# State product of each group issued one z piece ahead, with five smaller moves in the order of VectorE, ScalarE and GpSimd

## The reference, cut to what matters

```python
u = rms_norm(h, norm_mix)
z, xbc, dt_raw, q_a, c_kv, k_rope, gate_ssd, gate_mla = split_cols(u @ w_in)
# xbc: convolution, silu, split into xs (2048), B and C (4 groups x 128)
# 4 groups of 8 heads of 64, 2 chunks of 128 tokens:
cb      = C . B                          # per group and chunk, 128 x 128
y_diag  = (cb * exp(a_cum_l - a_cum_s) for s <= l) . (x * dt)
state   = B . (decay_to_end * x * dt)    # of chunk 0, 128 x 512 per group
y_off   = exp(a_cum) * C . state         # into chunk 1
y       = (y_diag + y_off + d_skip * x) * silu(z)
y       = y * rsqrt(mean(y * y per group) + eps) * ssd_norm
y_ssd   = y @ w_ssd_out
merged  = sigmoid(gate_ssd) * y_ssd + sigmoid(gate_mla) * y_mla
```

## Time and profile before

| | |
|---|---|
| median of 3 runs | 1092.04 us (1090.55 to 1095.19) |
| the profiled execution's own time | 1089.01 us |
| its span, first to last instruction | 1087.2 us |
| PE busy | 1011.7 us, 93% of the span |
| DVE, ACT, POOL busy | 621.3, 517.4, 19.4 us |
| mean granted TensorE clock | 0.981 |
| the stage of the change, end of z 1 to start of so 1 | 113.2 to 212.3 us of the span |

### The profile page before, as it was taken

How to read it: one execution, slowest core, us unless ns; L and a number is a source line. 1 busy time by engine, 2 the same in 40 slices (tenths; PEclk the granted TensorE clock), 3 DMA queues, 4 the chain that set the end, 5 groups by cost and what they waited for, 6 DMA issues and landing times.

```text
span 1087.2 us, 19436 instructions
## 1 busy us (share of the span) xinstructions
PE 1011.7 (93%) x8574; PEld 932.8 (86%) x8574; DVE 621.3 (57%) x828; ACT 517.4 (48%) x701; POOL 19.4 (2%) x24
## 2 busy tenths in 40 slices
PE   7999989899999999999997768699999999999998
PEld 6999878799889999998765545389999999999998
DVE  6798677765565893544111110079994765555566
ACT  5576577745556573542211110168567563443453
POOL 0000020001000000000000000000000000000000
PEclk9999999999999999998999888899999999999999
DMA  7666342346224456499999999775320366555431
GB/s 280 249 221 228 117 188 91 148 166 233 78 78 162 171 197 251 168 387 381 412 420 420 422 419 421 310 294 194 127 107 34 132 232 210 183 190 194 169 141 40
DMA packets 34872, 240.97 MB, mean 222 GB/s; under 512 B 4064, under 2 KB 4448, under 8 KB 6368
## 3 DMA queue, kind: packets, MB, share of 16 engines
q1 hardware_dynamic: 33264, 232.54, 56.0%
q0 software_dynamic: 1232, 6.99, 1.7%
q10 hardware_dynamic: 288, 0.15, 0.1%
HBM read 238.58 MB, written 1.08 MB: 220 GB/s over the span
## 4 chain that ended last, share of the span: by engine, by line
PE 69%; DMA 11%; DVE 11%; ACT 6%; issue 2%; SPq 1%; DVEq 0%; ACTq 0%
PE ps L462 16%; PE ps L463 16%; PE ps L464 16%; DMA wr<-in_c_weights 8%; DVE wlo L1976 4%; PE ps L535 3%; PE ps L1225 3%; DMA T<-in_c_weights 2%; ACT whi L1324 2%; PE ps L1191 1%; PE ps L928 1%; DMA raw<-in_c_weights 1%; SPq L2945 1%; PE ps L1252 1%; PE ps L1265 1%
## 5 line engine op out<-in xcount | busy, mean ns | idle before, releaser
L1976 DVE TENSOR_TENSOR wlo<-raw,whi 128x2048 fp32r<-128x2048 f32 (+1 forms) x119 | 269.4, 2267 | 134.2 <-ACT whi L1324 134.0
L462 PE MATMUL ps<-XUh,whi 128*128 128x256 f32 x992 | 280.8, 283 | 8.6 <-DVE wlo L1976 7.7
L463 PE MATMUL ps<-XUl,whi 128*128 128x256 f32 x992 | 276.9, 279 | 0.0
L464 PE MATMUL ps<-XUh,wlo 128*128 128x256 f32 x992 | 276.9, 279 | 0.0
L1324 ACT ACTIVATE whi<-raw 128x2048 fp32r<-128x2048 f32 (+1 forms) x119 | 223.5, 1882 | 64.0 <-PE ps L464 61.6
L462 PEld LDWEIGHTS ps<-XUh,whi 128*128 128x128 f32 x992 | 188.6, 190 | 10.7 <-issue 8.3
L463 PEld LDWEIGHTS ps<-XUl,whi 128*128 128x128 f32 x992 | 187.4, 189 | 0.3
L464 PEld LDWEIGHTS ps<-XUh,wlo 128*128 128x128 f32 x992 | 187.0, 189 | 0.0
L1225 PE MATMUL ps<-wr,Xg 128*32 128x256 f32 x480 | 55.2, 455 | 20.1 <-DMA wr<-in_c_weights 10.9
L2867 DVE SCALAR_TENSOR_TENSOR sphs<-sphs,wsl,ps 128x256 f32<-128x256 f32 x8 | 3.8, 481 | 94.7 <-ACT sphs L1941 94.7
L1225 PEld LDWEIGHTS ps<-wr,Xg 128*32 128x32 f32 x480 | 29.2, 130 | 32.4 <-issue 28.6
(11 more groups left out here) (621 smaller groups left out, 2368.7 us busy)
## 6 DMA issues: line engine op xcount, KB each, us to landing
raw<-in_c_weights SPq DMA_DIRECT2D x139, 1024.0 KB, 4.9
wr<-in_c_weights SPq DMA_DIRECT2D x36, 1024.0 KB, 26.3
xhi<-in_c_weights SPq DMA_DIRECT2D x12, 1024.0 KB, 26.0
xlo<-in_c_weights SPq DMA_DIRECT2D x12, 1024.0 KB, 26.4
extra<-in_c_weights SPq DMA_DIRECT2D x10, 1024.0 KB, 27.4
acb<-sums POOLq DMA_DIRECT2D x4, 1024.0 KB, 4.7
T<-in_c_weights SPq DMA_DIRECT2D x4, 1024.0 KB, 24.8
T8b<-in_c_weights SPq DMA_DIRECT2D x4, 1024.0 KB, 26.0
```

The costliest lines, as they stand in the source:

```text
L462: pe.matmul(ps, h(k), xh(k), start=start and k == 0, stop=False, skip_group_check=loose)
L463: pe.matmul(ps, h(k), xl(k), start=False, stop=False, skip_group_check=loose)
L464: t = pe.matmul(ps, l(k), xh(k), start=False, stop=stop and k == kt - 1, skip_group_check=loose)
L1976: dve.tensor_tensor(l[:, 0:n], r, h[:, 0:n].bitcast(F32), ALU.subtract).then_inc(*did("w_lo", "split", i))
```

## The change

- PE: `s0 g` is issued after z 2g+2 instead of after z 2g+3, for groups 0 to 2. Group 3 keeps its place.
- DVE: for groups 1 and 2 the state copy moves ahead of the products `M` by `CB`; for groups 0 and 3 it keeps its place. The lower half `upcoming("z", 2g+1)` moves ahead of `CB` for groups 1 to 3.
- ACT: the table load stands ahead of the wait for `dte`; the silu of groups 0 and 1 (`gate_y(0)`) comes one step later, behind the upper half of z 6 and the evacuation of z 4; `ya_root(3)` comes ahead of the upper half of so 1.
- DVE: `ya_add(2)` comes ahead of the lower half of gs 3.
- POOL: the product of group 1 waits for `m0` of group 2 too.

```diff
@@ pe_program, ssd @@
                 t.then_inc(*did("ssd_pe", "cb", g))
                 yield
-                yield
                 ps, free = bank.take("s0", g)
                 w.wait_ge(*free)
                 w.wait_ge(*at_("ssd", "xw", g))
                 w.wait_ge(*at_("emptied", "btok"))
                 pe.matmul(ps[:, :], Btok[:, g, :], xw[:, :]).then_inc(*did("ssd_pe", "s0", g))
+                yield
                 if g == 3:
                     yield
@@ act_program, ssd @@
             for g in range(4):
+                table(LOGEXP)
                 w.wait_ge(*at_("ssd", "dte_in", g))
-                table(LOGEXP)
...
                 act.activation(M[:, 1, :, :], M[:, 1, :, :], ACT.Exp, scale=-1.0).then_inc(*did("ssd_act", "ssd", "e", g, 1))
+                yield
                 if g == 1:
                     gate_y(0)
-                yield
                 yield
@@ act_program @@
         ya_upper(2)
+        ya_root(3)
         upcoming("gate_ssd", 3)
-        ya_root(3)
         ya_upper(3)
@@ dve_program, ssd @@
+            def state(g):
+                w.wait_ge(*at_("s0", g))
+                dve.tensor_copy(S0[:, :], bank.ps("s0", g)[:, :]).then_inc(*bank.emptied("s0", g))
+
             for g in range(4):
+                if g:
+                    upcoming("z", 2 * g + 1)
                 w.wait_ge(*at_("cb", g))
...
                 t.then_inc(*did("ssd_dve", "ssd", "m0", g))
-                upcoming("z", 2 * g + 1)
+                if g == 0:
+                    upcoming("z", 1)
+                if g in (1, 2):
+                    state(g)
                 if g == 3:
                     ya_add(0)
                     ya_add(1)
...
                 yield
+                if g in (0, 3):
+                    state(g)
                 yield
-                w.wait_ge(*at_("s0", g))
-                dve.tensor_copy(S0[:, :], bank.ps("s0", g)[:, :]).then_inc(*bank.emptied("s0", g))
                 if g == 3:
                     yield
@@ dve_program @@
         ya_scale(1)
+        ya_add(2)
         upcoming("gate_ssd", 1)
-        ya_add(2)
@@ pool_program @@
             if g == 3:
                 gate_y(0)
+                w.wait_ge(*at_("ssd", "m0", 2))
                 gate_y(1)
```

## The result

The changed kernel took 1076.01 us in the median of 4 runs (1071.06 to 1078.36), the kernel before 1092.22 in 4 runs beside them: ratio 0.9851, 95% interval 0.9816 to 0.9887. The profiled execution took 1077.94 (span 1076.1) against 1089.01 (span 1087.2), so 11.1 less.

A forecast was written before the change was run, and what follows sets the result against it. Mostly bound by TensorE work, with only PE's waits to be gained: 1.25 + 2.15 + 2.90 + 1.42 + 0 + 1.49 = 9.2 us, so a median of 1092.0 − 9.2 = 1082.8 us, range 1079 to 1087.5.

The forecast's parts named there:

- Point 1: State product ahead, its copy ahead of M by CB: gains 1.25 us ahead of z 3 and 2.15 in y.
- −2.15 (1.74, 0.2, 0.2): Waits for the state copy inside y 1, y 0 and y 2, taken to go whole: 2.15 us gained.
- 16.25: One group's PE work without waits, in us, from two starts of the state product less a wait of 0.20.
- Point 2: Earlier lower half and table load, POOL's product of group 1 held: the wait ahead of z 7 goes, 2.90 us gained.
- Point 3: Half clock in z 7, behind the wait of 2.90, goes: 1.42 us gained, bounds 0 and 1.42.
- 7.8: Gain in us if the clock term is worth nothing and the rest holds, giving 1084.2; a rival at 15%.
- Point 4: `ya_add(2)` earlier: group sum 2 loses its 1.32 us wait, group sum 3 waits 1.65 instead of 0.33; net 0.
- Point 5: `ya_root(3)` ahead of the upper half of so 1: the 2.23 us wait in so 0 shrinks by 1.49, to 0.7.
- DVE did not become the bound in groups 1 and 2: Rival, 12%: state copy or POOL's product delays DVE in groups 1 and 2; 5.2 us gained, 1086.8.
- the tail did not give back: Rival, 10%: squares, roots and lower halves set so 0 whatever the order; 6.5 us gained, 1085.5.
- later stages absorbed nothing of the 11: Rival, 5%: the later memory-bound stage ends when it did before; 1 to 3 us gained, 1090.
- less half clock in the stage, not more: Rival, 3%: TensorE falls to half clock in the stage more often than before; slower, 1100 us with three pieces.

The follow-up runs named there:

- late_copy: Changed kernel with only the DVE state copies of groups 1 and 2 moved back behind the lower halves of z 6 and gs 0: stage 90.75 us against 88.03.
- no_lower: Changed kernel with the lower half put back behind M for groups 1 to 3: 1072.97 us in one run, stage 88.28.
- no_act_pool: Changed kernel with the table load, silu and POOL product moves undone, state product and lower half still early: 1085.49 us in one run, stage 93.25.
- no_root: Changed kernel with the root of group 3 back behind the upper half of so 1: 1075.37 us in one run, stage 89.50.
- packed: Changed kernel with the tail of the stage also reordered on ACT and DVE: 1075.04 us, ratio 0.9881 to the kernel before, stage 86.26.
- again_before: The kernel before, unchanged, run again with its own trace: ratio 0.9962 against itself, 12 runs with a median of 1088.25 us, stage 100.61.
- no_state: Changed kernel with the state product and its copy put back on PE and DVE: 1083.27 us, ratio 0.9923 to the kernel before, stage 91.92.
- only_state: Kernel before with only the moves of the state product and its copy: 1086.06 us, ratio 0.9928 to the kernel before, stage 93.67.

## Why the prediction was right or wrong

**Right: what the change does, and that it lasts.** The state product stands behind z 2, z 4 and z 6, no wait is left from z 3 to gs 1, the clock is full, `dte` takes 0.15 and no table load follows it. The 11.1 of the two profiled executions are kept to the end of the kernel.

**Point 1, the state product, was mis-sized: here the forecast failed in the profile.** "−1.25" is right. "−2.15 (1.74, 0.2, 0.2)" reads the brackets as the cost of the waits. They cost 2.14 + 1.13: `late_copy` shows 0.38 on top for each. The same 0.38 sat in the 16.25 us that I took for one group's work without waits: I took off the bracket of 0.20 alone. In the changed kernel two starts of the state product lie 15.66 apart. The trace of before held it already, since y 3, which waits for nothing, lasts 3.11 from first start to last end, and y 0 3.70 with a bracket of 0.20. I had compared the waits, not the blocks. So y 1 began 2.0 earlier and y 2 8.9 earlier, measured from cb 0, where the forecast had 1.4 and 7.7; y 0 began 1.2 earlier, as forecast.

**Point 2.** −2.90 came, and `M` by CB was held for 0.36 where I took 0.6. The reason I gave first, the earlier lower half, is worth only 0.25 (`no_lower`); the table load, the silu and the POOL product together carry 5.2 (`no_act_pool`). The additions of y 1 took 0.48 each, under POOL's product and outside it, so 0 for them was right.

**Point 3, the half clock, was right for this profile, and one draw of several.** No half clock is left in the stage. The −1.42 itself was not measured apart; by the spacing of z 7 it is 1.4 to 1.6. I set the sum against the median as if all executions of before had one fall there, and gave the Trainium skill's rule only the chance of a smaller gain, 7.8. Three traces show that the kernel before has three waits behind which the clock may fall in the stage, and that one, two or three of them did: stages of 99.12, 100.27 and 100.61. The changed kernel has none of them, in four traces. The rule of the Trainium skill (TensorE: Matmul & The Clock Gate, part 1) that the gate follows recent activity, counted from instants that don't follow the kernel, agrees with that; I had applied it in one direction only. The mean gain of the stage is 12.0, but at the start of the expert stage it is 11.0, so the further falls of the stage don't explain the median in these traces.

**Point 4.** 0 was right: group sum 2 lost its 1.32 and group sum 3 waits 1.73 instead of 0.33, where 1.65 was forecast. No run undoes this move alone.

**Point 5.** −1.49 was forecast, the wait inside so 0 went from 2.23 to 0.75, and `no_root` costs 1.47.

**Not in the sum at all:** the 0.67, of which some 0.4 is the cheaper state product of groups 1 and 2 and the rest the chance of the spacing, and the small wait at group sum 0, 0.22.

**From 11 to the median.** 9.2 + 1.13 + 0.67 + 0.1 for the small waits is 11.1, and that is what the two profiled executions differ by. Over all runs, 53 of before have a median of 1091.4 and 17 of the changed kernel 1077.9, so 13.4 less. The 2.4 between the 11.0 at the expert stage and these 13.4 I can't place. Single runs spread by 12 us in the one and by 10 in the other, and the first four of the changed kernel, 1076.01, lay 2.6 below the median of its thirteen later ones. So of the 16.2 between the first medians 11 are shown to be the stage, and 2.8 are gone again when all runs are taken. With 11.1 in place of 9.2 the forecast would have been 1081, inside the range. What put the time outside it is the step from the sum of one profile to a median. The low end, 1079, was made from point 4 and part of the waits left in place, with no room for a wait that costs more than its bracket, and it took the scatter from three runs, 4.6, where seventeen show 12.4.

**The rivals.** None came. DVE did not become the bound in groups 1 and 2 (y 2 waits for nothing), the tail did not give back, later stages absorbed nothing of the 11, and there was less half clock in the stage, not more. But the 1 us or so beyond the 11, and the 1.8 of `packed`, did not reach the expert stage.

## What to carry to other kernels

Price a wait by the block that it stands in, with and without the wait, not by its bracket: among small matmuls a wait of 0.2 us cost 0.6. Where the clock falls behind a wait in the one trace you have, count every wait of that size as one behind which it may fall, and look at several traces before you set a sum against a median; and follow the difference to a later point of the kernel, since what `again_before` lost to the clock in one stage was made good by the expert stage. When a product is made earlier, ask what its inputs now stand behind: with the state product and the lower half early, but table load, silu and GpSimd's product where they were, it waited 2.33 us for its `xw`, and the stage took 5.2 more.

## What the runs showed of the hardware

- A wait inside a run of 64-column products cost 0.37 to 0.39 us beyond its bracket, for brackets from 0.20 to 1.74 (kernel before, `no_state`, `late_copy`, `only_state`). 0.28 of it is there at the first matmul behind the wait; the bracket begins at the recorded end of the matmul before, 0.27 behind its start, where the next one else starts 0.05 behind (`late_copy`).
- At full granted clock the same weight piece of 48 matmuls runs at 0.113 or at 0.118 us a matmul (z 6: 5.61 us in the first trace of before, 5.43 in that of the changed kernel). I found no cause.
- Behind waits of 1.94 to 3.09 us TensorE was granted 1.2 GHz for some 3.3 us (once for 6.7, the 0.72 of the stretch from 156 to 168) in some executions and not in others of the same kernel. Behind a wait of 2.48 both happened within one execution (`only_state`). Behind the waits of 1.73 to 1.84 of this stage no trace shows a fall.
- Identical kernels measured 0.9962 (0.9938 to 0.9985) against each other: 0.4% is not a finding here.
- GpSimd's product of 1024 columns took 2.40 alone and 4.39 when a VectorE instruction with two inputs in SBUF had started 0.16 before it; in the other order VectorE's 128x8 `dte` took 2.03 instead of 0.15.
